# A denser order of the side work in a two-lane schedule, and a gate multiplied in another order

## The chip, the cores and the metric

One core of a Trainium2 chip runs the whole program in one launch. The metric is the device time of that launch in microseconds (us). TensorE multiplies, VectorE and ScalarE do the elementwise work, GpSimd a little of it, and SyncE issues the loads of the weights.

## The reference

Four layers over one sequence of 256 tokens with 2048 features, all in float32. The change touches the last of them (called layer 3 here), which reads, cut to its core:

```python
def odd_layer(x, norm_g, w_in, ...):
    proj = rmsnorm(x, norm_g) @ w_in
    xc, zc, qd, kd, vd, zd, a_pre, b_pre = split_cols(proj, OD_SIZES)
    xconv = causal_dwconv(xc.astype(f32), conv_c_w.astype(f32)) + conv_c_b.astype(f32)
    yc = rg_lru(xconv, gate_w, gate_b, lam) * jax.nn.silu(zc.astype(f32))
    qkv = jax.nn.silu(causal_dwconv(jnp.concatenate([qd, kd, vd], axis=-1).astype(f32), conv_d_w.astype(f32)))
...
    q = l2norm(q.reshape(b, s, H_D, HD_D))
    k = l2norm(k.reshape(b, s, H_D, HD_D))
...
    od = gated_delta_chunkwise(q, k, v, beta, g)
    yd = rmsnorm(od, onorm_g).reshape(b, s, W_D) * jax.nn.silu(zd.astype(f32))
    y = jnp.concatenate([yc, yd], axis=-1).astype(x.dtype)
    return y @ w_out

def rg_lru(xconv, gate_w, gate_b, lam):
...
    log_a = -C_RG * r * jax.nn.softplus(-lam.astype(jnp.float32))
    a = jnp.exp(log_a)
    inp = jnp.sqrt(-jnp.expm1(2.0 * log_a)) * (i * xconv)
...
    _, hs = lax.associative_scan(combine, (a, inp), axis=1)
```

The convolutions have four taps. `gated_delta_chunkwise` needs the inverse of a lower triangular matrix; the kernel gets it in blocks of 128 by six levels of doubling. silu(z) is computed as z/2 * (1 + tanh(z/2)). The result of the layer is added to x.

## The kernel before, in words

**The projections.** Every large product is done in three passes to hold float32 accuracy: the weights are split by ScalarE into a high part (a cast, line 1099) and by VectorE into a low part (a subtraction, line 1659, which waits for the cast), and TensorE multiplies high by high, high by low and low by high (lines 557 to 559). One weight tile of 128x1024 is a *half*; TensorE does 12 matmuls of 512 columns per half, in four triples. In layer 3 there are twelve projections of 32 triples each (384 triples), then the last product.

**The side work.** All else of layer 3 is written as generators, one per engine, that yield between their steps. TensorE's loop calls `next(side)` after each triple; ScalarE's and VectorE's loops call it four times per half too. The calls are numbered, here called places; a step named for place p is issued by every engine at place p of its own instruction order. There is no other order than this written one: an engine that has to wait at a step waits with all that it has behind it, the casts and subtractions for the projections included. Those are issued three halves ahead of their use (`AHEAD = 3`), at every fourth place.

**The lanes.** `lanes` (line 99) starts the generators: three lists of (place, generator), and an entry starts when its place is reached and the entry before it in its list has ended. The first list holds the gates' vectors, lru(0), lru(2), delta(0), delta(2); the second lru(1), lru(3), delta(1), delta(3); the third the four parts of the gate, gated(0) to gated(3), which only VectorE runs. Each list has its own buffers (`Lane`) and two PSUM banks. Within a generator, `to(step)` yields until that step. `wide_steps(lane)` stretches the steps of an lru by 4/3 in the first lane and by 6/3 in the second, rounded down; an lru has 32 steps. A delta has 115.

**An lru's steps** (its line on each engine): transposes at 0 (TensorE); copy at 1, first tap at 3 (ScalarE, 1491 and 1496); three tap pairs at 4, 6 and 8 (VectorE, 2124); the gate product "g" at 11 (TensorE, 953); two Tanh pairs at 12, two Exp pairs "A" at 15, Tanh "th" at 18, Sqrt at 23 (ScalarE, 1505, 1517, 1517, 1521; Tanh and Exp share a function table, Sqrt has another); products at 15 and 20, product and two scans at 25 (VectorE, 2141, 2146, 2150, 2154); transposes "st" at 28 (TensorE, 959); a copy to y at 30.

**A delta's steps:** transposes of q, k, v at 0 and 4 (597), copies and first taps on ScalarE from 0 to 7 (1537, 1546), nine tap pairs on VectorE from 4 to 22, the three Tanh at 10, 16 and 24 (1562); squares at 23 and their sums "ss" by one-column matmuls at 27 (987); a decay product at 30 (993), the decay block on VectorE at 32 (2193 to 2196), its exponentials at 34 (1568), u at 36 (2210); k times k at 42 (1002), "ad" at 43 and 45 (six of line 2220), q times k at 48 (1008), "tq" at 49 (2225, 2226), the transposes at 53 (1015) and 56, six levels of two steps each three places apart (972 on TensorE, 2233 on VectorE, 1580 and 1583 on ScalarE); u0, a10, u1 and o from 96 to 105 (1038 to 1055), and the normalized result to y by 114 (2261).

**Arrivals.** At the end of each projection ScalarE copies the result out of PSUM (line 1205, or 1639 for the gate's Tanh), between the side steps of two halves: x at places 32 and 64, q and k at 96, 160, 192 and 256, v at 128 and 224, z at 288, 320, 352 and 384. The projections alternate between two pairs of PSUM banks; `free` says what TensorE waits for before it overwrites a pair.

Of the kernel before, what the change touches and what calls it, by code (L numbers as in the profile page):

```python
# [10 lines left out]
ALU = mybir.AluOpType  # L11
# [72 lines left out]
def wide_steps(lane):  # L84

    to = steps()
    return lambda step: to(step * (4, 6)[lane] // 3)
# [71 lines left out]
def build_program(nc, a, out, layers=(0, 1, 2, 3)):  # L159
    assert tuple(layers) == (0, 1, 2, 3)  # L160
    ctx = ExitStack()
    with ctx:
# [107 lines left out]
        z3_a, z3_d = marks("z3_a", "tanh"), marks("z3_d", "z mul")  # L270
# [274 lines left out]
        def tensor(pe):  # L545
# [418 lines left out]
            def delta(pair):  # L964
# [34 lines left out]
                yield from to(42)  # L999
# [5 lines left out]
                yield from to(48)  # L1005
# [5 lines left out]
                yield from to(53)  # L1011
# [5 lines left out]
                yield from to(56)  # L1017
# [6 lines left out]
                for l in range(1, 7):  # L1024
                    yield from to(53 + 6 * l)
                    pe.wait_ge(*da.at(r, f"mt{l - 1}"))
                    four_by_four(b, v.AD, v.Mt).then_inc(*dp.up(f"z{l}"))
                    yield from to(56 + 6 * l)
# [11 lines left out]
                yield from to(99)  # L1040
# [4 lines left out]
                yield from to(102)  # L1045
# [4 lines left out]
                yield from to(105)  # L1050
# [8 lines left out]
                yield from to(115)  # L1059

            def delta_gates():
# [18 lines left out]
                    qk3_a.at(2, "qk"), v3_a.at(1, "v"), qk3_a.at(3, "qk"), z3_d.at(0, "z"), z3_d.at(1, "z")]  # L1080
# [5 lines left out]
            last_product(3, side, [yt_d.at(29, "lo"), z3_d.at(3, "z")], [], [z3_d.at(3, "mul")], fine=True)  # L1086


        def scalar(act):
# [438 lines left out]
            def delta(pair):  # L1528
# [41 lines left out]
                yield from to(53)  # L1570
# [3 lines left out]
                yield from to(56)  # L1574
                act.wait_ge(*dp.at(r, "mt"))
                act.copy(flat(v.Mt), ps[:, b, :]).then_inc(*da.up("mt0"))
                for l in range(1, 7):
                    yield from to(56 + 6 * l)
# [5 lines left out]
                yield from to(107)  # L1584
                act.wait_ge(*dd.at(r, "od"))
                act.activation(v.B, v.Z, ACT.Square).then_inc(*da.up("osq"))
                yield from to(115)
# [63 lines left out]
        def vector(dve):  # L1651
# [506 lines left out]
            def delta(pair):  # L2158
# [53 lines left out]
                for hh, bank in ((0, b + 1), (1, b)):  # L2212
                    yield from to(43 + 2 * hh)
# [9 lines left out]
                yield from to(49)  # L2223
# [3 lines left out]
                yield from to(50)  # L2227
                dve.wait_ge(*dg.at(r, "diag"))
                dve.tensor_tensor(v.M, v.AD, bc(L3.lev[:, 0], 1, 4), ALU.mult).then_inc(*dd.up("m"))
                for l in range(1, 7):  # L2230
                    yield from to(53 + 6 * l)
# [4 lines left out]
                yield from to(96)  # L2236
                dve.wait_ge(*dp.at(r, "u0"))
                dve.tensor_copy(v.u[:, :, 0], two(b)).then_inc(*dd.up("u0"))
                yield from to(99)
                dve.wait_ge(*dp.at(r, "a10"))  # L2240
                dve.tensor_tensor(v.u[:, :, 1], v.u[:, :, 1], two(b + 1), ALU.subtract).then_inc(*dd.up("a10"))
                yield from to(102)
                dve.wait_ge(*dp.at(r, "u1"))
                dve.tensor_copy(v.u[:, :, 1], two(b)).then_inc(*dd.up("u1"))
                yield from to(105)
# [3 lines left out]
                yield from to(109)  # L2249
# [4 lines left out]
                yield from to(112)  # L2254
                dve.wait_ge(*dg.at(r, "opow"))
                dve.tensor_tensor(v.Z, v.Z, bc(sc[:, 28:32], 2, P), ALU.mult).then_inc(*dd.up("on"))
                yield from to(114)
# [6 lines left out]
                yield from to(115)  # L2264
# [64 lines left out]
            def gated(n):  # L2329
# [15 lines left out]
                m.then_inc(*z3_d.up("mul"))  # L2345

# [6 lines left out]
        def gpsimd(pool):  # L2353
# [109 lines left out]
            def delta(pair):  # L2463
# [9 lines left out]
                yield from to(46)  # L2473
# [3 lines left out]
                yield from to(110)  # L2477
                pool.wait_ge(*dd.at(r, "omean"))
                pool.tensor_tensor(sc[:, 28:32], sc[:, 28:32], nhalf[:, 0:4], ALU.pow).then_inc(*dg.up("opow"))
                yield from to(115)  # L2480
# [52 lines left out]
```

## Time and profile before

| | |
|---|---|
| median of 3 runs | 2524.33 us (2523.95 to 2525.02) |
| profiled execution | 2524.33 us, its span 2522.6 us |
| mean granted TensorE clock | 0.991 |
| TensorE busy | 2470.3 us |
| VectorE, ScalarE, GpSimd busy | 1382.7, 1233.0, 125.0 us |
| layer 3's projections | from 2031.66 us on |

Times are from the span's start. "Busy" for TensorE counts pipelined matmuls, whose ends are modelled; a matmul of 512 columns is listed with 0.39 us though the next starts 0.23 us after it. What an engine waited for is inferred from semaphores.

### The profile page before, as it was taken

What the parts mean: (1) busy time and instruction counts of PE and PEld (TensorE: products, weight loads), DVE (VectorE), ACT (ScalarE), POOL (GpSimd) and SP (SyncE); (2) the same over time, 40 slices, a digit from 0 to 9 for tenths busy, and PEclk for the clock granted to TensorE, in tenths of its full rate; (3) what the DMA queues carried; (4) which work ended last, traced back from release to release, by engine and by line L of the source; (5) the groups of instructions that cost most, each with busy time, mean ns of one, the idle gap of its engine ahead of it and who ended that gap; (6) DMA issues with size and microseconds to landing.
All of it is one profiled execution on the core that took longest, in us unless ns stands there. A gap on an engine that the chain in (4) does not pass through costs nothing.

```text
span 2522.6 us, 30023 instructions
## 1 busy us (share of the span) xinstructions
PE 2470.3 (98%) x12030; PEld 2060.6 (82%) x12030; DVE 1382.7 (55%) x1848; ACT 1233.0 (49%) x1661; POOL 125.0 (5%) x125
## 2 busy tenths in 40 slices
PE   8999999999999999989999989999999999999999
PEld 6888888888888888868888868888888887888887
DVE  5645454645464646554545565555445466746554
ACT  4454444444454445344555345555444368645443
POOL 1101010101010101000000000000000000000000
PEclk9999999999999999989999989999999999999999
DMA  7545555555555554635533545555555555433344
GB/s 239 188 159 185 166 184 167 181 164 173 171 172 175 183 167 151 217 125 187 180 117 116 186 143 177 174 184 173 182 173 164 179 184 161 137 103 117 101 134 134
DMA packets 342048, 414.49 MB, mean 164 GB/s; under 512 B 19019, under 2 KB 269093, under 8 KB 341397
## 3 DMA queue, kind: packets, MB, share of 16 engines
q1 hardware_dynamic: 340500, 405.63, 50.3%
q0 software_dynamic: 1408, 6.94, 0.7%
q8 instruction: 95, 1.56, 0.3%
q14 instruction: 45, 0.36, 0.0%
HBM read 410.42 MB, written 2.10 MB: 164 GB/s over the span
## 4 chain that ended last, share of the span: by engine, by line
PE 92%; DVE 3%; ACT 3%; issue 1%; SPq 0%; DMA 0%; POOL 0%; DVEq 0%; ACTq 0%
PE ps L557 26%; PE ps L559 26%; PE ps L558 26%; PE ps L972 2%; PE ps L597 2%; PE ps L712 1%; DVE wlo L1659 1%; ACT whi L1099 1%; PE ps L699 1%; PE ps L773 1%; PE ps L704 1%; PE ps L772 1%; PE ps L785 0%; PE ps L696 0%; DVE x L1758 0%
## 5 line engine op out<-in xcount | busy, mean ns | idle before, releaser
L1659 DVE TENSOR_TENSOR wlo<-raw,whi 128x1024 fp32r<-128x1024 f32 (+1 forms) x774 | 950.3, 1233 | 858.0 <-ACT whi L1099 854.8
L557 PE MATMUL ps<-whi,xh 128*128 128x512 f32 (+1 forms) x3072 | 1227.4, 400 | 6.7 <-DVE wlo L1659 6.7
L559 PE MATMUL ps<-whi,xl 128*128 128x512 f32 (+1 forms) x3072 | 1198.0, 390 | 0.0
L558 PE MATMUL ps<-wlo,xh 128*128 128x512 f32 (+1 forms) x3072 | 1195.8, 389 | 0.0
L1099 ACT CAST whi<-raw 128x1024 fp32r<-128x1024 f32 (+1 forms) x774 | 801.6, 1041 | 771.3 <-PE ps L559 766.7
L557 PEld LDWEIGHTS ps<-whi,xh 128*128 128x128 f32 x3072 | 578.6, 188 | 123.0 <-issue 12.2
L559 PEld LDWEIGHTS ps<-whi,xl 128*128 128x128 f32 x3072 | 577.6, 188 | 120.4
L558 PEld LDWEIGHTS ps<-wlo,xh 128*128 128x128 f32 x3072 | 578.9, 188 | 109.7
L1177 ACT ACTIVATE work<-work,small 128x128 f32<-128x128 f32 (+1 forms) x80 | 46.1, 577 | 155.7 <-DVE small L1769 155.7
L2387 POOL TENSOR_TENSOR work<-work 128x512 f32<-128x512 f32 x48 | 77.0, 1605 | 872.4 <-DVE work L1844 488.6
L972 PEld LDWEIGHTS ps<-work 128*128 128x128 f32 x544 | 67.7, 191 | 6.1 <-DVE work L2233 2.6
L972 PE MATMUL ps<-work 128*128 128x128 f32 x544 | 68.7, 275 | 1.3 <-DVE work L2233 1.2
L1240 ACT COPY work<-ps 128x512 f32<-128x512 f32 x48 | 28.2, 587 | 65.0 <-PE ps L597 65.0
L597 PE MATMUL ps<-ident,x 128*128 128x128 f32 x128 | 25.7, 377 | 31.0 <-DVE x L1758 17.7
L1766 DVE CUSTOM_DVE_ANT_0 work<-ps,work 128x128 f32<-128x128 f32 (+1 forms) x80 | 38.2, 514 | 31.3 <-PE ps L699 17.5
L597 PEld LDWEIGHTS ps<-ident,work 128*128 128x128 f32 x352 | 42.8, 140 | 9.6
L597 PE MATMUL ps<-ident,work 128*128 128x128 f32 x352 | 50.4, 272 | 0.0
L597 PEld LDWEIGHTS ps<-ident,x 128*128 128x128 f32 x128 | 22.0, 198 | 34.7 <-DVE x L1758 27.3
L1279 ACT COPY work<-ps 128x1024 f32<-128x1024 f32 x32 | 32.4, 1012 | 27.4 <-PE ps L559 27.4
L1205 ACT ACTIVATE work<-ps,rstd 128x512 f32<-128x512 f32 (+3 forms) x56 | 28.3, 561 | 29.2 <-PE ps L559 28.6
L1183 ACT COPY work<-ps 128x384 f32<-128x384 f32 (+1 forms) x40 | 29.5, 736 | 26.3 <-PE ps L704 17.4
L2124 DVE SCALAR_TENSOR_TENSOR work<-work,vec 128x256 f32<-128x256 f32 x96 | 41.9, 480 | 0.3
(366 smaller groups left out, 1319.9 us busy)
## 6 DMA issues: line engine op xcount, KB each, us to landing
raw<-in_dsa_w_in SPq DMA_DIRECT2D x320, 512.0 KB, 4.5
raw<-in_ev_w_in SPq DMA_DIRECT2D x144, 512.0 KB, 4.6
raw<-in_od_w_in SPq DMA_DIRECT2D x96, 512.0 KB, 4.5
raw<-in_mla_w_in SPq DMA_DIRECT2D x48, 512.0 KB, 4.3
raw<-in_dsa_w_out SPq DMA_DIRECT2D x32, 512.0 KB, 4.6
raw<-in_mla_w_out SPq DMA_DIRECT2D x32, 512.0 KB, 4.7
raw<-in_ev_w_out SPq DMA_DIRECT2D x32, 512.0 KB, 4.6
raw<-in_od_w_out SPq DMA_DIRECT2D x32, 512.0 KB, 4.9
```

Source lines behind the costliest of these rows:

```text
L557: pe.matmul(o, xh[:, k, tokens[tb]], hi, start=start and s + l == 0, stop=False)
L558: pe.matmul(o, xh[:, k, tokens[tb]], lo, start=False, stop=False)
L559: m = pe.matmul(o, xl[:, k, tokens[tb]], hi, start=False, stop=stop and s + l == 2)
L597: m = pe.transpose(ps[:, bank, i * P:(i + 1) * P], src(i // 2, i % 2), ident[:, :])
L972: m = pe.matmul(ps[:, bank, n * P:(n + 1) * P], left[:, n, :], right[:, n, :], start=True, stop=True)
L1099: act.copy(whole_half(whi[:, h % 4], widths[u]), whole_half(raw[:, u % 4, 2 * (h % 2):2 * (h % 2) + 2], widths[u])).then_inc(hi_done, 1)
L1177: m = act.activation(w, w, ACT.Exp, bias=nb[:, tb:tb + 1], scale=scale, accum_out=den[:, tb:tb + 1])
L1279: act.copy(L0.h[:, 2 * s:2 * s + 2].rearrange("p b t c -> p t b c"), ps[:, b:b + 2, :].rearrange("p t (b c) -> p t b c", b=2)).then_inc(*e ...
L1659: dve.tensor_tensor(whole_half(wlo[:, h % 4], n), whole_half(raw[:, h // 2 % 4, 2 * (h % 2):2 * (h % 2) + 2], n), whole_half(whi[:, h % 4] ...
L1766: m = dve.tensor_tensor_reduce(w_, s_, m_, 1.0, LOWEST, ALU.add, ALU.max, mx[:, tb:tb + 1])
L2124: return dve.scalar_tensor_tensor(out=out_, in0=src[:, L3.PAD - 3 + j:L3.PAD - 3 + j + S], scalar=w, in1=out_, op0=ALU.mult, op1=ALU.add)
L2387: pool.tensor_tensor(L0.t1, L0.h[:, blk].rearrange("p t (h d) -> p (t h) d", h=2), L0.cosa, ALU.mult).then_inc(*p0_g.up(f"cos{n}"))
```

## The change

Four edits, all in layer 3, none of which changes what is computed:
- the second lane's lru is stretched by 5/3 instead of 6/3 (53 places instead of 64), and its two start at 44 and 101 instead of 48 and 114;
- in every delta, the steps after 36 are moved forward: by 2 from the product of k and k on, by 3 from the q and k transposes through the levels, by 4 from u0 on, so that it has 111 places;
- delta(1), delta(2) and delta(3) start at 164, 244 and 276 instead of 180, 250 and 298;
- the gate: before, (tanh + 1) * z goes to a scratch tile and is then multiplied by hrstd and y, one token block at a time. After, (tanh + 1) * y is written to y, and then z out of PSUM is multiplied by hrstd and y. PSUM is so released by the last operation instead of the first, and the Tanh's scratch tile by the first instead of the last. The extra delay of 25 places ahead of gated(3)'s last operations goes.

```diff
-    return lambda step: to(step * (4, 6)[lane] // 3)
+    return lambda step: to(step * (4, 5)[lane] // 3)
...
-    lane = [[(0, gates()), (40, lru(0)), (86, lru(2)), (132, delta(0)), (250, delta(2))],
-            [(48, lru(1)), (114, lru(3)), (180, delta(1)), (298, delta(3))],
+    lane = [[(0, gates()), (40, lru(0)), (86, lru(2)), (132, delta(0)), (244, delta(2))],
+            [(44, lru(1)), (101, lru(3)), (164, delta(1)), (276, delta(3))],
...
-                yield from to(42)
+                yield from to(40)
                 pe.wait_ge(*dd.at(r, "u"))
...
-                yield from to(48)
+                yield from to(46)
                 pe.wait_ge(*dd.at(r, "ad1"))
...
-                yield from to(53)
+                yield from to(50)
                 pe.wait_ge(*dd.at(r, "tq"))
...
-                    yield from to(53 + 6 * l)
+                    yield from to(50 + 6 * l)
...
-                yield from to(96)
+                yield from to(92)
...
-                yield from to(115)
+                yield from to(111)
...
-                    qk3_a.at(2, "qk"), v3_a.at(1, "v"), qk3_a.at(3, "qk"), z3_d.at(0, "z"), z3_d.at(1, "z")]
+                    qk3_a.at(2, "qk"), v3_a.at(1, "v"), qk3_a.at(3, "qk"), z3_d.at(0, "mul"), z3_d.at(1, "mul")]
...
-                    act.wait_ge(*z3_d.at(turn - 1, "mul"))
+                    act.wait_ge(*z3_d.at(turn - 1, "add"))
...
-                dve.wait_ge(*z3_a.at(n, "tanh"))
-                dve.scalar_tensor_tensor(out=L3.scratch, in0=L3.scratch, scalar=1.0, in1=ps[:, b:b + 2, :],
-                                         op0=ALU.add, op1=ALU.mult).then_inc(*z3_d.up("z"))
-                yield from turns(25 if n == 3 else 1)
                 for i in range(2):
                     dve.wait_ge(*(rg_a[i].at(n, "end") if n < 2 else dl_d[i].at(n - 2, "fin")))
-                dve.wait_ge(*z3_d.at(n, "z"))
+                dve.wait_ge(*z3_a.at(n, "tanh"))
+                dve.scalar_tensor_tensor(out=y[:, :, c], in0=L3.scratch, scalar=1.0, in1=y[:, :, c],
+                                         op0=ALU.add, op1=ALU.mult).then_inc(*z3_d.up("add"))
                 for tb in range(TB):
                     yield
-                    m = dve.scalar_tensor_tensor(out=y[:, tb, c], in0=L3.scratch[:, tb], scalar=hrstd[:, tb:tb + 1],
+                    yield
+                    dve.wait_ge(*z3_d.at(n, "add"))
+                    m = dve.scalar_tensor_tensor(out=y[:, tb, c], in0=ps[:, b + tb, :], scalar=hrstd[:, tb:tb + 1],
                                                  in1=y[:, tb, c], op0=ALU.mult, op1=ALU.mult)
-                    yield
                 m.then_inc(*z3_d.up("mul"))
+                yield
```

The steps of ScalarE, VectorE and GpSimd in a delta are moved by the same numbers as TensorE's.

## Rows read from the trace of the kernel before

**Rows 1.** the page: span, and busy time of each engine with its share
```profile
span 2522.6 us, 30023 instructions
...
PE 2470.3 (98%) x12030; PEld 2060.6 (82%) x12030; DVE 1382.7 (55%) x1848; ACT 1233.0 (49%) x1661; POOL 125.0 (5%) x125
```

**Rows 2.** TensorE waits of layer 3: line waited for, total us, times, longest
```profile
PE ps L953 <- DVE work L2124: 2.4, 2, 1.2
PE ps L1008 <- DVE work L2220: 2.1, 1, 2.1
PE ps L987 <- ACT work L1559: 1.4, 1, 1.4
PE ps L1055 <- DVE work L2244: 1.2, 1, 1.2
PE ps L972 <- DVE work L2233: 1.2, 2, 0.6
```

**Rows 3.** timeline of TensorE: start us, us, instruction, idle before in brackets
```profile
2079.01 0.39 PE L557 MATMUL ps<-whi,xh 128*128 128x512 f32 x1
...
2085.13 1.99 PE L953 MATMUL ps<-work 128*128 128x256 f32 x8 [1.20 <-DVE work L2124]
...
2091.09 0.39 PE L557 MATMUL ps<-whi,xh 128*128 128x512 f32 x1
...
2092.18 0.66 PE L959 MATMUL ps<-ident,work 128*128 128x128 f32 x4 [0.25 <-DVE work L2154]
...
2192.29 0.48 PE L557 MATMUL ps<-whi,xh 128*128 128x512 f32 x1
```

**Rows 4.** timeline of ScalarE between places 56 and 72
```profile
2075.18 1.28 ACT L1505 ACT_TABLE_LOAD   x1
2076.47 0.47 ACT L1505 ACTIVATE work<-ps,work 128x256 f32<-128x256 f32 x1
...
2078.85 2.09 ACT L1517 ACTIVATE work<-work 128x256 f32<-128x256 f32 x4
2080.83 1.26 ACT L1205 ACTIVATE work<-ps,rstd 128x512 f32<-128x512 f32 x2
...
2082.91 1.11 ACT L1517 ACTIVATE work<-work 128x256 f32<-128x256 f32 x2
...
2084.97 1.28 ACT L1521 ACT_TABLE_LOAD   x1
```

**Rows 5.** timeline of VectorE, same stretch
```profile
2088.99 1.23 DVE L1659 TENSOR_TENSOR wlo<-raw,whi 128x1024 fp32r<-128x1024 f32 x1 [2.18 <-ACT whi L1099]
...
2090.86 1.27 DVE L2154 TENSOR_TENSOR_SCAN work<-work 128x256 f32<-128x256 f32 x2
```

**Rows 6.** busy time by stretch; the column after POOL is the granted clock
```profile
2160.30:2163.70 3.40, 3.40 (x10) 2.20 (x8) 1.93 (x4) 3.30 (x4) 0.60 (x1) 0.54 0.22 84
```

**Rows 7.** VectorE groups by form from 2028 to 2470 us
```profile
L1659 DVE TENSOR_TENSOR wlo<-raw,whi 128x1024 fp32r<-128x1024 f32 x112 | 137.3, 1226 | 121.3 <-ACT whi L1099 120.3 <-DVE work L2334 0.4
L2124 DVE SCALAR_TENSOR_TENSOR work<-work,vec 128x256 f32<-128x256 f32 x96 | 41.9, 480 | 0.3
...
L2220 DVE SCALAR_TENSOR_TENSOR work<-ps,small,work 128x128 f32<-128x128 f32 x24 | 6.8, 343 | 2.4 <-PE ps L1003 2.4
L2342 DVE SCALAR_TENSOR_TENSOR y<-work,hrstd,y 128x512 f32<-128x512 f32 x8 | 6.0, 746 | 0.1
...
L2154 DVE TENSOR_TENSOR_SCAN work<-work 128x256 f32<-128x256 f32 x8 | 5.1, 679 | 0.1
L2334 DVE SCALAR_TENSOR_TENSOR work<-work,ps 128x1024 f32<-128x1024 f32 x4 | 4.8, 1212 | 0.0
```

**Rows 8.** ScalarE groups by form from 2028 to 2470 us
```profile
L1099 ACT CAST whi<-raw 128x1024 fp32r<-128x1024 f32 x113 | 118.7, 1050 | 99.5 <-PE ps L559 99.0
...
L1546 ACT ACTIVATE work<-work,vec 128x256 f32<-128x256 f32 x24 | 10.5, 506 | 0.0
...
L1568 ACT ACTIVATE work<-work 128x128 f32<-128x128 f32 x16 | 5.9, 391 | 1.4 <-DVE work L2196 1.4
```

More of the change, by code:

```diff
@@ L269, in build_program @@
         x3_a, qk3_a, v3_a = marks("x3_a", "x"), marks("qk3_a", "qk"), marks("v3_a", "v")
-        z3_a, z3_d = marks("z3_a", "tanh"), marks("z3_d", "z mul")
+        z3_a, z3_d = marks("z3_a", "tanh"), marks("z3_d", "add mul")
         rg_a = [marks(f"rg_a{i}", "cp c0 gate A asq th sqrt end") for i in range(2)]
@@ L1016, in delta @@
                 m.then_inc(*dp.up("tr"))
-                yield from to(56)
+                yield from to(53)
                 pe.wait_ge(*da.at(r, "st"))
@@ L1024, in delta @@
                 for l in range(1, 7):
-                    yield from to(53 + 6 * l)
+                    yield from to(50 + 6 * l)
                     pe.wait_ge(*da.at(r, f"mt{l - 1}"))
                     four_by_four(b, v.AD, v.Mt).then_inc(*dp.up(f"z{l}"))
-                    yield from to(56 + 6 * l)
+                    yield from to(53 + 6 * l)
                     pe.wait_ge(*dd.at(r, f"z{l}"))
@@ L1039, in delta @@
                 m.then_inc(*dp.up("u0"))
-                yield from to(99)
+                yield from to(95)
                 pe.wait_ge(*dd.at(r, "u0"))
@@ L1044, in delta @@
                 m.then_inc(*dp.up("a10"))
-                yield from to(102)
+                yield from to(98)
                 pe.wait_ge(*dd.at(r, "a10"))
@@ L1049, in delta @@
                 m.then_inc(*dp.up("u1"))
-                yield from to(105)
+                yield from to(101)
                 pe.wait_ge(*dd.at(r, "u1"))
@@ L1085, in tensor @@
                         then=turning_y(3, [[z3_d.at(2, "mul")], [], [], [], [], []]) if n == 11 else None)
-            last_product(3, side, [yt_d.at(29, "lo"), z3_d.at(3, "z")], [], [z3_d.at(3, "mul")], fine=True)
+            last_product(3, side, [yt_d.at(29, "lo"), z3_d.at(3, "mul")], [], [z3_d.at(3, "mul")], fine=True)
         def scalar(act):
@@ L1569, in delta @@
                 m.then_inc(*da.up("ex"))
-                yield from to(53)
+                yield from to(50)
                 act.wait_ge(*dp.at(r, "tr"))
@@ L1573, in delta @@
                 act.copy(v.TRN[:, 1], ps[:, b, :]).then_inc(*da.up("st"))
-                yield from to(56)
+                yield from to(53)
                 act.wait_ge(*dp.at(r, "mt"))
@@ L1577, in delta @@
                 for l in range(1, 7):
-                    yield from to(56 + 6 * l)
+                    yield from to(53 + 6 * l)
                     act.wait_ge(*dp.at(r, f"t{l}"))
@@ L1583, in delta @@
                         act.copy(flat(v.M), ps[:, b + 1, :]).then_inc(*da.up(f"m{l}"))
-                yield from to(107)
+                yield from to(103)
                 act.wait_ge(*dd.at(r, "od"))
                 act.activation(v.B, v.Z, ACT.Square).then_inc(*da.up("osq"))
-                yield from to(115)
+                yield from to(111)
             def delta_gates():
@@ L2212, in delta @@
                 for hh, bank in ((0, b + 1), (1, b)):
-                    yield from to(43 + 2 * hh)
+                    yield from to(41 + 2 * hh)
                     if hh == 0:
@@ L2222, in delta @@
                     m.then_inc(*dd.up(f"ad{hh}"))
-                yield from to(49)
+                yield from to(47)
                 dve.wait_ge(*dp.at(r, "qk"))
@@ L2226, in delta @@
                 dve.tensor_tensor(v.TRN[:, 1, P:], ps[:, b, 0:3 * P], v.E[:, 1], ALU.mult).then_inc(*dd.up("tq"))
-                yield from to(50)
+                yield from to(48)
                 dve.wait_ge(*dg.at(r, "diag"))
@@ L2230, in delta @@
                 for l in range(1, 7):
-                    yield from to(53 + 6 * l)
+                    yield from to(50 + 6 * l)
                     dve.wait_ge(*dp.at(r, f"z{l}"))
@@ L2248, in delta @@
                                   ALU.mult).then_inc(*dd.up("od"))
-                yield from to(109)
+                yield from to(105)
                 dve.wait_ge(*da.at(r, "osq"))
@@ L2253, in delta @@
                 dve.tensor_scalar(sc[:, 28:32], sc[:, 24:28], 1.0 / P, EPS, ALU.mult, ALU.add).then_inc(*dd.up("omean"))
-                yield from to(112)
+                yield from to(108)
                 dve.wait_ge(*dg.at(r, "opow"))
                 dve.tensor_tensor(v.Z, v.Z, bc(sc[:, 28:32], 2, P), ALU.mult).then_inc(*dd.up("on"))
-                yield from to(114)
+                yield from to(110)
                 dve.wait_ge(*dd.at(r, "on"))
@@ L2263, in delta @@
                                   ALU.mult).then_inc(*dd.up("fin"))
-                yield from to(115)
+                yield from to(111)
             def delta_gates():
@@ L2472, in delta @@
                 pool.tensor_tensor(sc[:, 0:8], sc[:, 0:8], nhalf[:, 0:8], ALU.pow).then_inc(*dg.up("pow"))
-                yield from to(46)
+                yield from to(44)
                 pool.wait_ge(*dd.at(r, "ad1"))
@@ L2476, in delta @@
                                    pattern=[[0, 4], [-1, P]], channel_multiplier=1).then_inc(*dg.up("diag"))
-                yield from to(110)
+                yield from to(106)
                 pool.wait_ge(*dd.at(r, "omean"))
                 pool.tensor_tensor(sc[:, 28:32], sc[:, 28:32], nhalf[:, 0:4], ALU.pow).then_inc(*dg.up("opow"))
-                yield from to(115)
+                yield from to(111)
             run(lanes(lambda: nothing, delta, lru, lambda n: nothing))
```

8 lines of the change are left out of this document (4 added, 4 removed).

## The prediction

> **What bounds the kernel now.** I read the page first: TensorE is busy for 2470.3 of 2522.6 us [rows 1]. The change adds and removes no TensorE instruction, so it can move the time only through TensorE's waits and its clock. The profiled execution took 2524.33 us, its span and 1.73 us around it; that is also the median of the three runs, so no correction is needed.
>
> Next come TensorE's waits in layer 3, the only layer that is touched. They add up to 8.3 us in five lines of the view [rows 2]; shorter ones, the 0.25 of L959 in [rows 3] among them, bring them to 8.9 us. The reader is to see that each is a wait for a small VectorE or ScalarE result that a side chain delivers late. The third thing is the clock. Behind the 1.4 us wait for the squares (L987), TensorE shows a granted clock of 0.54 for 3.4 us [rows 6]: it ran at 1.2 GHz where it otherwise runs at 2.4, which costs about half of 3.4, or 1.6 us. So at most 8.9 + 1.6 = 10.5 us can be won, and what can be lost has no such bound.
>
> How the side chains are paced: a *place* is what lies between two triples of projection matmuls. A triple takes 0.68 us (2091.09 begins triple 77; L959 follows it after one triple and a wait of 0.25) [rows 3], so four places, one half, take 2.72 us plus side matmuls. I write T(n) for the start of triple n; T(64) is 2079.01 [rows 3]. In each half ScalarE owes a cast of 1.05 us [rows 8] and VectorE a subtraction of 1.23 us that waits for that cast [rows 7]. Everything else is in the engines' program order around these, so a ScalarE backlog reaches every later VectorE operation through the subtraction: its 112 instances waited 120 us for the cast [rows 7].
>
> **The change part by part.** The four edits are: the lru lanes 1 take 53 instead of 64 places and start at 44 and 101 (were 48 and 114); each delta takes 111 places (was 115); the second delta of a pair starts 32 places behind the first (was 48); and the gate is multiplied in another order.
>
> *Gate.* It stays one 128x1024 operation of 1.21 us and two of 128x512 of 0.75 us [rows 7]. TensorE's wait for bank release moves from the first to the last of them, four places later. At place 294 that is 26 places ahead of its use at 320. Cost zero; if that cover were gone it would be at most 0.75 + 0.75 us. The 25-place delay of the fourth gate goes, but TensorE shows no wait at its late transposes (place 424) before, so nothing is won there. The order of the Tanh and the last multiplication also shows no wait now. Zero.
>
> *Place 77, lru(0) with lru(1).* Before, ScalarE does at places 56 to 70: table load and gates of lru(0) (ends 2078.0), cast, A of lru(0), arrival of x, cast, th, cast, then table load and sqrt, which ends at about 2086.9 [rows 4]. Now lru(1) has its gate product at place 62, its gates at 64 and its A at 69, in front of that sqrt. T(64) becomes 2079.01 + 1.9 (the eight gate matmuls, L953 [rows 3]) = 2080.9. ScalarE, full throughout: th(0) ends 2084.1, gates(1) +1.5 = 2085.6, cast 2086.6, A(1) +2.0 = 2088.6 (four L1517 [rows 4]), sqrt(0) +1.9 = 2090.5, cast of place 72: 2091.5. Before, the chain from the start of VectorE's subtraction (2088.99) to TensorE's release (2092.18) took 3.2 us: subtraction, product, two scans [rows 3, 5]. So it is released at 2094.7. It gets there at 2080.9 + 14 x 0.68 = 2090.4. Wait: 4.3 us, where 1.2 + 0.25 stood.
>
> *Place 100, lru(2).* Arrival of qk, cast, subtraction, taps are unchanged; only lru(1)'s sqrt no longer sits in front (it held the arrival for 0.45 us). 1.17 becomes 0.75.
>
> *Place 147, lru(3) with delta(0).* Count from T(120) = 0, when lru(3)'s gate product is done. ScalarE: gates 2.4, cast 3.8 (not before T(124) = 2.7), end(2) 4.4, A(3) 6.4, arrival of v 7.9, cast 8.9, th(3) 9.9, cast 10.9, two copies 11.9, four first taps at 0.4 apiece 13.5 [rows 8], cast 14.5, copy and taps of v 15.9, table load and sqrt 17.8, cast 18.9. VectorE: subtraction 20.05, two tap pairs of 0.8 (two L2124 overlap) 21.65, product and scans 1.9 [rows 7] = 23.5. TensorE: 28 places x 0.68 = 19.0, plus st(2), eight and four transposes (0.55 + 0.95 + 0.5) = 21.05. Wait: 2.4 us. What is behind the waiting instruction on TensorE is its whole projection.
>
> *Places 159 to 178.* Following the same queues, delta(0)'s squares come 0.4 us late (1.4 before), its decay product waits 1.3 us for VectorE's subtraction behind the arrival of qk. Then delta(1), now starting at 164, brings its taps into delta(0)'s middle. In program order ScalarE has from T(164): cast 1.05, two copies 2.2; the exponentials cannot start before VectorE's decay block (3.3) and take 1.9 (six L1568 [rows 8]) = 5.25; four taps 6.9; cast 8.0. VectorE: subtraction 9.2, u 9.8. TensorE asks for u at place 40 of the delta (was 42), at 8.1 to 8.4: wait 1.4 to 1.7, I take 1.4. Two taps pairs, subtraction, taps and six L2220 later, ad1 ends 0.8 us behind the request. Sum 0.4 + 1.3 + 1.4 + 0.8 = 3.9; the 0.16 for lru(3) at place 171 goes.
>
> *Places 276 to 304.* The second pair meets the same, and gated(0) at 290 falls between delta(2)'s ad1 and its tq. From place 276 to 300 VectorE owes: 6 subtractions at 1.15 = 6.9; delta(3)'s nine tap pairs 7.2 and two products 1.2; delta(2)'s decay block, scalings and u 2.1, six ad 1.7, tq and m 1.5; the gate 2.5: 23.1 us. TensorE needs 24 x 0.68 = 16.3 and about 5 of side matmuls, 21.3. Placed in order, the waits are 1.4 (u), 0.9 (ad1), 1.4 (tq, behind the 1.2 us gate) and 1.1 (the first level). Sum 4.8, where 2.1 stood (L1008) [rows 2].
>
> *The rest.* The 1.2 for u1 behind the subtraction (L1055) and the two of 0.6 for the levels (L972) have equivalents after, but one of the 0.6 is already counted in the 1.1 above: 2.4 before, 1.8 after.
>
> Sum of waits after: 4.3 + 0.75 + 2.4 + 3.9 + 4.8 + 1.8 = 17.95; before 8.9: +9.05. Clock: the dip of 1.6 us at 2160 stood behind a wait and sixteen one-column matmuls; with a wait of 0.4 there I let it go: -1.6. A 4.3 us wait at place 77 may draw one of its own (the 2.1 us wait drew none), unknown from the rows: 0 to 1.6, I take 0. Total +7.45 us: **2531.8**. Bounds: with every overlap of queues a little kinder (each new wait down by two thirds) it is about +1; with two dips of 1.6 +10.7.
>
> One rule speaks for a higher price. In the rows a switch of ScalarE's functions costs 1.28 us and the activation starts 0.01 us behind the load (2075.18 + 1.28 to 2076.47) [rows 4]. The Trainium skill ("ScalarE: Activation LUTs", What ACT_TABLE_LOAD costs) says that each switch has a drain besides and comes to about 2.66 us. By that, the two switches ahead of place 77 and the two ahead of 147 would each add up to 1.4 us and the forecast would be some 5 us more, as an estimate; the trace contradicts it, so it is not in the sum.
>
> **The rivals.**
> *A. The backlogs are absorbed (no change).* The side work has slack: before, VectorE idled 121 us in front of its subtractions [rows 7]. If my queues are each 1.5 to 2 us too pessimistic, seven waits shrink to about the old 9 us and the time is 2522 to 2527. Against it: ScalarE's 56 to 72 is an ordered queue with no idle between 2075 and 2087 [rows 4], and 3.5 us are inserted in it.
> *B. Faster.* The collisions of before go: lru(3)'s tail no longer lies on delta(0) at 160 to 171 (1.4 + 0.2 + the 1.6 of clock), the gate no longer on delta(1)'s end at 290 to 299 (2.1), u1 (1.2). With new waits under 1.5 us in all: 2524.3 - 6.5 + 1.3 = about 2519. It decides if the new overlaps at 69 and 284 fit; my tables say they don't.
> *C. The clock falls.* Waits of 4.3 and 2.4 us in succession draw two or more dips of 1.6 us, and they are not hidden: 2535 and above.
>
> **How the numbers follow.** A measurement of this kernel tells about 0.2% (5 us) from no change. Forecast (2528 to 2535): 0.56. A: 0.27. B: 0.11. C: 0.06. The range that leaves out no more than 2 in 10 takes in A and most of the forecast: 2522 to 2536; the forecast's own is 2528 to 2535. The forecast of 7.5 us lies 2.5 above the bound, so a little of it counts as the same: slower 0.59, same 0.30, faster 0.11.
>
> **What would show it.** In the profile after: a wait of 3.5 to 5 us of L959 for L2154 near 2090; one of 1.5 to 3.5 us of L959 near 2150; waits of L1002 for L2210 and of L1008 for L2220 in both pairs, L1015 for L2226 near 2310; no 1.2 GHz stretch near 2160; no wait on y or z. It is wrong if the sum of TensorE's waits in layer 3 is below 12 us, above all if ScalarE runs sqrt(0) before 2089.

## The result and the profile after

The changed kernel takes 2545.61 us (median of 4, 2540.57 to 2546.34) against 2524.59 us: ratio 1.0078, 95% interval 1.0066 to 1.009. (The ratios in this document come with the runs. They are not the quotient of the two medians, which is 1.0083 here; the two differ by up to 0.0008.) It is slower by 21 us, where 2531.8 us (range 2522 to 2536) had been forecast. The profiled execution has a span of 2544.0 us.

The page of the changed kernel, the lines that answer to [rows 1]:

```profile
span 2544.0 us, 30020 instructions
...
PE 2480.8 (98%) x12030; PEld 2067.7 (81%) x12030; DVE 1382.0 (54%) x1848; ACT 1232.2 (48%) x1661; POOL 123.7 (5%) x125
```

The same 12030 matmuls, but TensorE's busy time grew by 10.5 us. Waiting cannot do that; slower matmuls can. Its waits in layer 3, the view of [rows 2] (waiting line, releaser, us in total, times, longest):

```profile
PE ps L959 <- DVE work L2154: 6.6, 2, 4.2
PE ps L972 <- DVE work L2233: 3.5, 2, 2.3
PE ps L1002 <- DVE work L2210: 3.1, 2, 1.9
PE ps L1043 <- DVE work L2238: 2.1, 2, 1.5
PE ps L1015 <- DVE work L2226: 1.2, 1, 1.2
PE ps L953 <- DVE work L2124: 0.9, 1, 0.9
PE ps L597 <- DVE y L2342: 0.9, 1, 0.9
...
PE ps L987 <- ACT work L1559: 0.3, 1, 0.3
PE ps L1008 <- DVE work L2220: 0.3, 1, 0.3
```

These are 18.9 us against 8.9 before: +10.0. The clock is the other half. Busy time by stretch of the changed kernel, for the four stretches of layer 3 in which the column after POOL, the granted clock, stands at half:

```profile
2093.40:2100.30 6.90, 4.74 (x13) 3.89 (x14) 3.90 (x6) 3.23 (x6) 0.00 (x0) 0.51 0.48 152
2168.50:2175.30 6.80, 6.80 (x17) 4.32 (x16) 1.90 (x3) 1.61 (x2) 2.08 (x2) 0.50 0.50 157
2322.10:2325.50 3.40, 3.40 (x11) 2.75 (x10) 3.40 (x8) 0.57 (x1) 0.00 (x0) 0.51 0.82 292
2346.00:2356.20 10.20, 10.20 (x42) 9.33 (x40) 2.00 (x3) 2.12 (x3) 2.03 (x1) 0.50 0.32 103
```

TensorE is busy for 4.74 + 6.80 + 3.40 + 10.20 = 25.1 us of them at 1.2 instead of 2.4 GHz, which costs half of it, 12.6 us. Before there was one such stretch of 3.4 us [rows 6], worth 1.7. So +10.9 us, and with the waits +20.9; the spans differ by 21.4, of which 0.95 stood before layer 3 began.

The place of the largest wait, read as in [rows 3 to 5]: TensorE, ScalarE and VectorE of the changed kernel (start, us, instruction, idle before it).

```profile
2081.71 0.39 PE L557 MATMUL ps<-whi,xh 128*128 128x512 f32 x1
...
2095.56 1.11 PE L959 MATMUL ps<-ident,work 128*128 128x128 f32 x4 [4.17 <-DVE work L2154]
...
2096.90 0.63 PE L558 MATMUL ps<-wlo,xh 128*128 128x512 f32 x1
```

```profile
2084.01 1.09 ACT L1517 ACTIVATE work<-work 128x256 f32<-128x256 f32 x2
2085.00 0.47 ACT L1505 ACTIVATE work<-ps,work 128x256 f32<-128x256 f32 x1
...
2087.36 2.10 ACT L1517 ACTIVATE work<-work 128x256 f32<-128x256 f32 x4
2089.48 1.28 ACT L1521 ACT_TABLE_LOAD   x1
2090.77 0.63 ACT L1521 ACTIVATE work<-work 128x512 f32<-128x512 f32 x1
```

```profile
2092.37 1.22 DVE L1659 TENSOR_TENSOR wlo<-raw,whi 128x1024 fp32r<-128x1024 f32 x1 [3.01 <-ACT whi L1099]
...
2094.23 1.27 DVE L2154 TENSOR_TENSOR_SCAN work<-work 128x256 f32<-128x256 f32 x2
```

Up to here the whole program lies 0.95 us later than before; all of that stood already at layer 3's first triple (2032.61 instead of 2031.66), so it is not the work of the moved steps. ScalarE does th(0), at once the gates of lru(1), the cast, and four exponentials, and only then loads the table for sqrt(0), at 2089.48 where before it did so at 2084.97 [rows 4]. VectorE's subtraction of place 72 starts at 2092.37, the scans follow, and TensorE is released at 2095.56 after 4.17 us; the forecast was 4.3. The clock fell at 2093.4, about 2 us into the wait. The matmul at 2096.90 shows what comes with it: 0.63 us instead of 0.39. The wait of 2.38 us at place 147 drew no such stretch.

The stretch at 2168.5 has no such wait near it. TensorE's timeline there:

```profile
2165.58 1.95 PE L987 MATMUL ps<-ones,work 128*128 128x1 f32 x16 [0.34 <-ACT work L1559]
2167.39 0.48 PE L557 MATMUL ps<-whi,xh 128*128 128x512 f32 x1
...
2169.12 0.63 PE L557 MATMUL ps<-whi,xh 128*128 128x512 f32 x1
...
2170.53 2.07 PE L993 MATMUL ps<-work,ident 8*128 8x256 f32 x4
```

It waited only 0.34 us, then did sixteen matmuls of one column, and about a microsecond later the clock was at half. That asks whether waits or small matmuls lower the clock.

### The profile page after: what moved, and what is told of

Read it like the earlier page. It is cut to its first block, busy times and chain, and to the rows that moved or that the text cites. A ratio compares the mean times of both kernels' runs of the same rounds, so it can differ in the third digit from the quotient of the medians.

```text
span 2544.0 us, 30020 instructions
## 1 busy us (share of the span) xinstructions
PE 2480.8 (98%) x12030; PEld 2067.7 (81%) x12030; DVE 1382.0 (54%) x1848; ACT 1232.2 (48%) x1661; POOL 123.7 (5%) x125
## 4 chain that ended last, share of the span: by engine, by line
PE 90%; DVE 4%; ACT 3%; issue 1%; DMA 0%; SPq 0%; POOL 0%; ACTq 0%; DVEq 0%
PE ps L557 26%; PE ps L559 26%; PE ps L558 26%; PE ps L972 2%; PE ps L597 2%; DVE wlo L1659 1%; PE ps L712 1%; ACT whi L1099 1%; PE ps L699 1%; PE ps L773 1%; PE ps L704 1%; DVE work L2124 1%; PE ps L772 1%; PE ps L785 0%; PE ps L696 0%
## 5 line engine op out<-in xcount | busy, mean ns | idle before, releaser
L972 PEld LDWEIGHTS ps<-work 128*128 128x128 f32 x544 | 69.1, 195 | 8.3 <-DVE work L2233 4.7
L972 PE MATMUL ps<-work 128*128 128x128 f32 x544 | 70.2, 279 | 3.5 <-DVE work L2233 3.5
L597 PE MATMUL ps<-ident,x 128*128 128x128 f32 x128 | 25.1, 367 | 31.5 <-DVE x L1758 17.7
L597 PEld LDWEIGHTS ps<-ident,x 128*128 128x128 f32 x128 | 21.1, 192 | 35.3 <-DVE x L1758 27.3
```

The lines of the kernel that those rows point to most:

```text
L597: m = pe.transpose(ps[:, bank, i * P:(i + 1) * P], src(i // 2, i % 2), ident[:, :])
L972: m = pe.matmul(ps[:, bank, n * P:(n + 1) * P], left[:, n, :], right[:, n, :], start=True, stop=True)
```

## The experiments

Theory W: the loss is 10 us of waits, made by what ScalarE's and VectorE's written order puts in front of the releasing operation (Q), and 11 us of clock that these waits draw. Rival D: crowded small matmuls lower the clock, whether or not TensorE waits. Each kernel is compared with the kernel before on the same chip; its median there was 2524.8 to 2526.1 us, so times of two experiments can differ by 1.3 us from the chip alone.

**1. The gate alone.** The new order of multiplications in parts 0 to 2 of the kernel before, part 3 as before.

```diff
-                dve.scalar_tensor_tensor(out=L3.scratch, in0=L3.scratch, scalar=1.0, in1=ps[:, b:b + 2, :],
-                                         op0=ALU.add, op1=ALU.mult).then_inc(*z3_d.up("z"))
...
+                dve.scalar_tensor_tensor(out=y[:, :, c], in0=L3.scratch, scalar=1.0, in1=y[:, :, c],
+                                         op0=ALU.add, op1=ALU.mult).then_inc(*z3_d.up("add"))
```

> The kernel before with the new order of the gate's multiplications in parts 0 to 2 (part 3 as before, since its first operation would otherwise wait for results that come later in VectorE's own order). Theory W (the 21 us are 10 us of new TensorE waits and 12 us of half clock drawn by them): the gate has no share, 2524.6 +/- 1 us, the waits of layer 3 near 8.9 us and one short stretch at 1.2 GHz. Rival G (PSUM released four places later holds a projection up): a wait on y of 1 us or more at places 320 or 352 and a time over 2526.

Measured: 2525.76 us, ratio 0.9998 (0.9989 to 1.0008); waits 8.7 us, no wait on y at 320 or 352. G falls. The profile has a second 3.4 us stretch at half clock near place 299, behind a wait (L1008, 1.9 us; 2.1 before) that drew none in the profile before, so such stretches differ between executions.

**2. The lru's lane alone.**

```diff
-    return lambda step: to(step * (4, 6)[lane] // 3)
+    return lambda step: to(step * (4, 5)[lane] // 3)
-            [(48, lru(1)), (114, lru(3)), (180, delta(1)), (298, delta(3))],
+            [(44, lru(1)), (101, lru(3)), (180, delta(1)), (298, delta(3))],
```

> The kernel before with the second lane's lru alone changed (5/3, starts 44 and 101). Theory W: waits of 4.2 us at place 77 and 2.4 at place 147 appear, 1.4 at 160 shrinks, and the clock falls to 1.2 GHz behind them for two stretches of 3 to 7 us: 2524.6 + 7.5 to 10, about 2531 to 2534. Rival D (the clock falls only where both lanes' small matmuls lie close together, mostly after place 160): the same waits but at most one short stretch, about 2528.

Measured: 2532.75 us, ratio 1.002 (1.001 to 1.003). Its waits on TensorE:

```profile
PE ps L959 <- DVE work L2154: 6.5, 2, 4.2
...
PE ps L987 <- ACT work L1559: 0.4, 1, 0.4
```

They are 4.16 us at place 77, 2.32 at 147 and 0.36 at 159. There are two stretches of 6.8 us at half clock, at the first and behind the third; the 2.32 us wait drew none. A third of the loss is here.

**3. Offset 48 between the deltas of a pair**, with the new lru and the new steps, and the old gate (the gate's lines are undone too).

```diff
-            [(44, lru(1)), (101, lru(3)), (164, delta(1)), (276, delta(3))],
+            [(44, lru(1)), (101, lru(3)), (180, delta(1)), (292, delta(3))],
```

> The changed kernel with the second delta of each pair 48 places behind the first instead of 32 (starts 180 and 292), and the old gate, which that needs. Theory W: the waits at 173, 192, 285, 295 and 304 (about 8 us) go or shrink to 3, and with them the two stretches at 1.2 GHz from 2320 on; the lru's share stays: 2532 to 2535. Rival S (the delta's own shorter steps make the waits, whatever the offset): waits of 5 us or more after place 160 remain, time over 2538.

Measured: 2533.88 us, ratio 1.0026 (1.0016 to 1.0037). After place 160 there are nine short waits, 0.4 to 0.9 us each, 5.0 us in all, and no half clock behind them. That sum is the sign that rival S named, but the kernel before has 4.9 us there too, against 11.0 in the changed kernel, and the time is under S's 2538: S falls. Over experiment 2 the shorter steps cost about 1 us, which is within the noise; the offset of 32 costs the rest: 2545.6 - 2533.9 = 11.7 us (the gate's order, which differs too, has no share, see 11).

**4. The changed kernel with its waits filled** by matmuls whose results nobody reads.

```diff
+            def fill(bank, n):
+                for _ in range(n):
+                    pe.matmul(ps[:, bank, :], xh[:, 0, 0:P], flat(xh[:, 0:2, :]), start=True, stop=True)
...
                 yield from to(28)
+                if pair in (0, 3):
+                    pe.wait_ge(*rg_a[i].at(r, "gate"))
+                    fill(b + 1, 18 if pair == 0 else 10)
                 pe.wait_ge(*rg_d[i].at(r, "scan"))
```

> The changed kernel with useless 512-column matmuls put where TensorE waits: 18 at place 77, 10 at 147, 5 and 8 ahead of the product of k and k in delta(0) and delta(2), 5 and 10 ahead of their first level. They fill about as long as the waits last. Theory W: the clock stays at 2.4 GHz at most of these places, time at 1.2 GHz in layer 3 falls from 27 us to 10 or less, the time to 2533 to 2539. Rival D (crowded small matmuls, not waits, lower the clock): the stretches at 1.2 GHz stay, 2545 or more.

The other fills stand ahead of L1002 and of the first level. Measured: 2537.21 us, ratio 1.0041 (1.0026 to 1.0056), 8.4 us less than the changed kernel with 56 more matmuls. Granted clock by stretch in this kernel, the place of the old 4.2 us wait and the one behind place 160:

```profile
2093.40:2100.30 6.90, 6.81 (x32) 5.38 (x31) 5.28 (x7) 4.86 (x7) 0.10 (x1) 1.00 0.46 152
2165.50:2168.90 3.40, 3.40 (x10) 2.65 (x9) 2.01 (x4) 1.55 (x3) 0.44 (x1) 0.52 0.27 105
```

The first is back at 2.4 GHz, and so are the two of the second pair; only 3.4 us behind the one-column matmuls are left. So in the three other places it took an idle TensorE to draw the half clock; the fourth fits rival D.

**5. The stretch of 5/3 with the old starts** (48 and 114).

```diff
-    return lambda step: to(step * (4, 6)[lane] // 3)
+    return lambda step: to(step * (4, 5)[lane] // 3)
```

> The kernel before with the stretch of 5/3 alone, the lru starts left at 48 and 114. Then only lru(1)'s gates (1.5 us), not its A (2.0 us), come in front of sqrt(0) in ScalarE's order. Theory Q (each wait is what ScalarE's and VectorE's written order puts in front of the releasing operation): the wait at place 77 is 4.2 - 2.0 = 2.2 us, the one at 147 moves to 160 with 1.5 to 3 us; time 2 to 5 us over before. Rival P (the shorter stretch itself leaves an lru too few places for its chain): the wait stands at lru(1)'s own steps, places 90 or later.

Measured: 2528.98 us, ratio 1.0007 (0.9998 to 1.0016). Waits:

```profile
PE ps L987 <- ACT work L1559: 3.5, 1, 3.5
...
PE ps L959 <- DVE work L2154: 1.9, 1, 1.9
```

The wait at 77 is 1.91 us, where taking the 2.0 us of exponentials out of ScalarE's way had forecast 2.2; the other moved to place 159 and is 3.5, above the 1.5 to 3 expected. Q holds, P falls.

**6. gated(0) at 304 in the changed kernel.**

```diff
-            [(290, gated(0)), (322, gated(1)), (354, gated(2)), (388, gated(3))]]
+            [(304, gated(0)), (322, gated(1)), (354, gated(2)), (388, gated(3))]]
```

> The changed kernel with gated(0) started at place 304 instead of 290. Theory Q: VectorE's 2.5 us of gate leave the rush of delta(2) and delta(3); the waits at 295 (1.2) and 304 (2.3) become those of the first pair, where no gate lies (0 and 1.15), so 2 to 3 us less of waits, and with the second pair's waits like the first's the clock falls for one stretch less; 2538 to 2543. Rival: the rush is set by ScalarE (exponentials and taps) and nothing changes, 2545.

Measured: 2537.27 us, ratio 1.0042 (1.0029 to 1.0054). The level waits (L972) come to 2.3 us, 1.15 in either pair, and L1015 waits no more: 2.4 us less, as Q said. In all the waits are 3.8 us less; the rest is the first pair's 1.25 us at L1002, which has nothing to do with the gate: it seems hidden because the half clock behind place 160 lasts 10.2 us in this profile, not 6.8, and makes TensorE late. The second pair's 10.2 us at half clock are gone, the 3.4 us ahead of them stay. The time lies just under the 2538 to 2543 expected: the collision of the gate with the pair is worth 8 us of the medians, more than its waits.

**7. A delay alone.** Six useless products before lru(0)'s scan, in the kernel before.

```diff
+                if pair == 0:
+                    for n in range(6):
+                        dve.tensor_tensor(flat(v.gt), flat(v.A2), flat(v.A2), ALU.mult).then_inc(dly, 1)
+                        dve.wait_ge(dly, n + 1)
                 dve.wait_ge(*ra.at(r, "sqrt"))
```

> The kernel before with six useless 128x512 VectorE products (0.7 us each, 4.1 in all, into a tile that is free) in front of lru(0)'s scan, and the order otherwise as before. It makes the wait at place 77 near 4 us without any crowding of small matmuls. Theory W: the clock falls to 1.2 GHz behind it, for one stretch of 3 to 7 us, costing 1.7 to 2.4 us beyond the wait; time +4 to +6.5 over before. Rival D: no stretch behind place 77, time +4 or less.

Measured: 2531.71 us, ratio 1.0019 (1.001 to 1.0028). The wait (L960 in this kernel's lines), and the stretch that TensorE resumes in:

```profile
PE ps L960 <- DVE work L2159: 4.6, 1, 4.6
```

```profile
2097.60:2101.00 3.40, 2.97 (x9) 2.56 (x10) 2.09 (x3) 0.00 (x0) 0.00 (x0) 0.52 0.00 0
```

TensorE stood still from 2093.42 to 2098.03 with only 512-column matmuls in the 4 us before, and the clock fell at about 2097.7. So a wait suffices, without small matmuls crowded about it. It fell about 4 us into this wait, and about 2 us into the one of 4.17 us in the changed kernel. The decay product waits too now, for 0.8 us. This profile has a third stretch of 3.4 us, at the 2.1 us wait of L1008, as in experiment 1. The ratio is small beside 6.5 us of medians; the executions of the kernel before themselves spread from 2523.6 to 2530.5 us there, with mean clocks from 0.992 to 0.989.

**8. The gaps of the layer normalizations filled** in the kernel before (36 and 14 matmuls in each).

```diff
             def turn_x(layer):
                 for g in range(8):
+                    if layer in (1, 2) and g == 0:
+                        pe.wait_ge(*add_d.at(layer - 1, "add2"))
+                        fill(0, 36)
+                    if layer in (1, 2) and g == 4:
+                        pe.wait_ge(*xt_a.at(8 * layer, "hi"))
+                        fill(0, 14)
```

> The kernel before with useless 512-column matmuls in TensorE's two long gaps at the layer normalizations: 36 (8.2 us) in each gap of 8.4 us and 14 in each of 3.6 us. Theory W: the two stretches of 17.1 us at 1.2 GHz (at 1087 and 1476) disappear or fall below 7 us; since most of what runs in them is transposes that wait for ScalarE and VectorE anyway, the time falls by 2 to 5 us. Rival: the clock falls whatever fills the gap, time within 1 us of before.

Measured: 2525.85 us, ratio 0.9998 (0.9989 to 1.0007), mean clock 0.995 to 0.998. TensorE in the first gap, and below it the same transposes in the kernel before:

```profile
1085.80 8.32 PE L597 MATMUL ps<-xh 128*128 128x512 f32 x36
1094.40 1.10 PE L601 MATMUL ps<-ident,x 128*128 128x128 f32 x8 [0.28 <-DVE x L1768]
1096.79 1.09 PE L601 MATMUL ps<-ident,x 128*128 128x128 f32 x8 [1.30 <-DVE x L1768]
```

```profile
1093.80 1.97 PE L597 MATMUL ps<-ident,x 128*128 128x128 f32 x8 [8.43 <-DVE x L1758]
1096.19 1.97 PE L597 MATMUL ps<-ident,x 128*128 128x128 f32 x8 [0.43 <-DVE x L1758]
```

Both stretches of 17 us at half clock are gone and the eight transposes take 1.1 instead of 1.97 us, but the next group starts 2.39 us after the first in both kernels, when VectorE's quarter of x is there: what the matmuls gained, the wait took (1.30 instead of 0.43 us). The clock was low where it did not matter: the mechanism as said, the gain forecast not.

**9. gated(0) at 304 in the kernel before.** The edit is that of 6.

> The kernel before with gated(0) moved from place 290 to 304. Theory Q (what stands ahead in VectorE's written order makes the wait): the 2.1 us wait at place 299 falls below 1 us and nothing else moves; 1 to 1.5 us under before, more where it also spares a stretch at 1.2 GHz. Rival: the wait is set by delta(1)'s end and stays, no difference.

Measured: 2528.57 us, ratio 1.0004 (0.9995 to 1.0013). Waits:

```profile
PE ps L972 <- DVE work L2233: 3.9, 3, 2.7
...
PE ps L1008 <- DVE work L2220: 0.4, 1, 0.4
```

L1008 fell from 2.1 to 0.4 us, and a wait of 2.71 us appeared at place 313, where delta(3)'s taps now meet the gate. Between 2324.7 us and the operation it waits for (2335.3), VectorE's timeline holds four pairs of delta(3)'s taps, two subtractions and the gate's three operations. This wait has 3.4 us at half clock with it. The wait had moved, not gone; "nothing else moves" was wrong.

**10. The kernel before with gated(0) at 304, the filled gaps, and 5, 5 and 6 matmuls at places 71, 101 and 160.** The edits of 8 and 9, and:

```diff
                 yield from to(11)
+                if pair in (1, 2):
+                    fill(b + 1, 5)
                 pe.wait_ge(*rg_d[i].at(r, "conv"))
...
                 yield from to(27)
+                if pair == 0:
+                    pe.wait_ge(*da.at(r, "cp1"))
+                    fill(b + 1, 6)
                 pe.wait_ge(*da.at(r, "sq"))
```

> The kernel before with gated(0) at 304, useless matmuls in the two gaps of the layer normalizations, and 5, 5 and 6 of them at the waits of places 71, 101 and 160. Theory W: mean clock 0.998, no stretch at 1.2 GHz in layer 3 in most executions, so 2519 to 2523, and less spread between executions. Rival: the filled places cost as much as they give, 2524 to 2527.

Measured: 2523.34 us, ratio 0.9992 (0.9983 to 1.0). Within what can be told from no change, and above the 2519 to 2523 expected; the 2.7 us wait of 9 is here too, with 3.4 us at half clock.

**11. The changed kernel with the old gate.** Starts and steps stay as changed, the gate's lines in the diff ahead of the prediction are undone.

> The changed kernel with the old order of the gate, starts and steps as changed. It takes the new gate apart from the offset of 32. Theory Q: the waits are the changed kernel's within 1 us and so is the time, 2543 to 2547, since the gate's operations take the same VectorE time at nearly the same places. Rival G: the new gate has a large share of the 11.7 us that lie between the offsets 48 and 32, time under 2540.

Measured: 2545.71 us, ratio 1.0073 (1.0059 to 1.0088), waits 19.0 us, 27.3 us at half clock. The gate's new order has no share.

**12. The one-column matmuls twice**, in the kernel before.

```diff
-                for n, m_ in enumerate((v.M, v.Mt)):
+                for n, m_ in 2 * list(enumerate((v.M, v.Mt))):
```

> The kernel before with the sixteen one-column matmuls that sum the squares issued twice in every delta (places 159, 207, 277, 325). It adds four times 1.6 us of small matmuls without adding a wait. Theory W in its strict form (only idle TensorE lowers the clock): +6.4 us, no new stretch at 1.2 GHz at 207, 277 and 325; about 2531. Rival D (matmuls of one column do as little for the clock as none): a stretch of 3 to 7 us behind each, 2536 or more.

Measured: 2540.04 us, ratio 1.0053 (1.0037 to 1.0068). The profile is of the longest of four executions, 2545.5 us; the others took 2539.4 to 2540.4, so it shows more half clock than they had. The waits are 8.7 us, unchanged. The timeline of TensorE around place 207, where nothing waits, and the clock behind places 159, 207 and 277:

```profile
2218.57 4.83 PE L987 MATMUL ps<-ones,work 128*128 128x1 f32 x32
2223.26 0.77 PE L557 MATMUL ps<-whi,xh 128*128 128x512 f32 x1
```

```profile
2162.90:2176.60 13.70, 13.70 (x38) 10.31 (x38) 5.22 (x10) 5.83 (x9) 2.02 (x1) 0.51 0.26 77
2220.90:2227.70 6.80, 6.80 (x27) 6.22 (x28) 0.39 (x2) 0.00 (x0) 1.65 (x1) 0.51 0.48 154
2309.70:2316.50 6.80, 6.80 (x23) 5.47 (x24) 2.08 (x4) 1.04 (x1) 2.02 (x1) 0.51 0.00 0
```

The strict form of W falls: at 207 the clock fell some 2 us after the first of the 32 began, with no wait near. But not behind every group, as D had it. At place 325 the same 32 took 3.63 us and the clock stayed up, and so it did in the kernel before at the three groups of sixteen that had no wait right ahead of them (2211, 2294 and 2350 us; the first is shown):

```profile
2369.33 3.63 PE L987 MATMUL ps<-ones,work 128*128 128x1 f32 x32
```

```profile
2210.61 1.84 PE L987 MATMUL ps<-ones,work 128*128 128x1 f32 x16
```

At full clock the added sixteen cost 3.63 - 1.84 = 1.8 us, four times 7.2; the other half of the 14 us between the medians is clock.

**13. The one-column matmuls in two eights**, one triple apart, in the kernel before.

```diff
                 for n, m_ in enumerate((v.M, v.Mt)):
+                    if n:
+                        yield from to(28)
                     for k in range(4):
```

VectorE's operation that waits for them moves from step 28 to 29.

> The kernel before with the sixteen one-column matmuls of each delta issued as eight at place 27 and eight at place 28, with a triple of wide matmuls between. Theory D2 (the clock falls where TensorE has little to do for some microseconds, by waiting or by one-column matmuls): the stretch of 3.4 us near place 160 stays, since the 1.4 us wait is there too, but the executions with a mean clock of 0.989 become rarer, median 0.5 to 2 us under before. Strict theory W: no difference.

Measured: 2524.66 us, ratio 0.9999 (0.999 to 1.0009). No difference: the 3.4 us stretch stays, as expected, but the slower executions do not become measurably rarer, where theory D2, that a TensorE with little to do lowers the clock, had a median 0.5 to 2 us lower.

**14. The kernel before with the split, the filled gaps and the fills at 71, 101 and 160.** The edits of 8, 10 (without gated(0)) and 13 together.

> The kernel before with the split of e13, the filled gaps of e8 and the fills at places 71, 101 and 160. Theory D2: mean clock 0.998 or 0.999 in nearly every execution, no stretch at 1.2 GHz near place 160 or 208, 2519 to 2523. Strict theory W: like e10, 2523.3.

Measured: 2523.63 us, ratio 0.9989 (0.998 to 0.9998). The lowest ratio of all, by 0.1% under before and not measurably under 10; it misses the 2519 to 2523 of D2. Its profile has no half clock near 160 or 208, but still 3.4 us at the 2.1 us wait of L1008, which was not filled.

**15. The changed kernel, filled and split.** The edits of 4 and 13 together.

> The changed kernel with the fills of e4 and the split of e13. Theory D2: the last stretch at 1.2 GHz of layer 3, behind place 160, goes too: 2534 to 2536.5 where e4 had 2537.2. What then lies over before is the waits (or their filling) alone, about 10 us. Strict theory W: 2537 as e4.

Measured: 2535.74 us, ratio 1.004 (1.0027 to 1.0053). Layer 3 of this kernel and, below it, of the changed kernel (granted clock after POOL):

```profile
2028.00:2500.00 472.00, 463.98 (x2499) 391.81 (x2498) 280.22 (x437) 255.22 (x379) 16.98 (x21) 1.00 0.42 132
```

```profile
2028.00:2500.00 472.00, 453.06 (x2404) 382.61 (x2402) 275.96 (x436) 252.35 (x377) 17.51 (x24) 0.97 0.41 128
```

The column is rounded, so the places of the old stretches of this kernel are shown closer:

```profile
2162.00:2182.00 20.00, 18.14 (x96) 14.38 (x95) 10.40 (x20) 13.20 (x25) 2.08 (x2) 1.00 0.43 125
2318.00:2358.00 40.00, 38.32 (x217) 32.18 (x216) 27.24 (x51) 16.79 (x28) 2.66 (x2) 1.00 0.33 105
```

There is no half clock left in layer 3. That is what the split adds to 4; in time the two can't be told apart (ratios 1.0040 and 1.0041, on two chips). What remains over before is 10.9 us, near the 10.0 of new waits. It isn't an exact sum: before has 1.7 us of clock that this kernel hasn't, and the 7.7 us of waits left plus the 56 filling matmuls (an estimate at 0.23 us each: 12.7) are 1.5 us more than the 18.9 that they replace.

## Why the prediction was wrong, point by point

- *The waits* were right in mechanism and, with some luck, in sum: 18.9 us against 17.95 forecast. Place 77: 4.17 (4.3). Place 100: 0.94 (0.75). Place 147: 2.38 (2.4). Places 159 to 178: 0.34, 0, 1.25 and 0.28 (0.4, 1.3, 1.4, 0.8); the decay product did not wait, since half clock had made TensorE late; without half clock there, in 15, it waited 0.75. The second pair: 1.87, 0, 1.19 and 2.33 (1.4, 0.9, 1.4, 1.1). Not foreseen were 1.15 at the first pair's level and 0.57 and 1.51 at L1043, the latter where the end of delta(1) meets the taps of delta(2); "the rest" had 1.8 and was these and 0.9 on y, 4.1 in all. So 2.0 us too much at 159 to 178 and 2.9 too little in the second pair and the rest nearly cancelled.
- *The step that failed* is the clock: "A 4.3 us wait at place 77 may draw one of its own [...]: 0 to 1.6, I take 0" and, for the stretch at place 160, "with a wait of 0.4 there I let it go: -1.6". It measured 12.6 us in place of 0, a change of +10.9 instead of -1.6. Two things were wrong in it. I priced a stretch by the one row at hand (3.4 us, 1.6 us of cost), but they lasted up to 10.2 us. And I let the stretch at 160 go with its wait: it stood behind a wait *and* sixteen one-column matmuls, and with 0.34 us of wait left it came all the same, 6.8 us long. Experiment 12 shows that one-column matmuls can lower the clock by themselves when there are 32 of them. With the measured waits and clock in its sum the forecast would be 2524.3 + 10.0 + 10.9 = 2545.2, so no other term of size was missing.
- *Rival C* (2535 and above) had the right mechanism with a chance of 0.06 and a price of 1.6 us a stretch; it should have been in the range. Rivals A and B fell with the waits. (The 2.1 us wait at 299 that B puts down to delta(1)'s end belongs to delta(2), which started at 250 and does its product of q and k at step 48.)
- *The gate at no cost*: right (1 and 11). That it collides with the second pair was right as well, but with the clock the collision costs 8 us, not the 2.5 of its two waits (6).
- *The load of an activation table* costs 1.28 us in the changed kernel too (2089.48), with nothing behind it. The price of the Trainium skill ("ScalarE: Activation LUTs", What ACT_TABLE_LOAD costs) is again not what the trace shows.
- *The signs in the profile* came as listed, except the wait of L1008 for L2220 (0.28 us in one pair), the stretch at 1.2 GHz that was not to be there near 2160 (it came at 2168), a wait on y of 0.9 us, and L1015, which came at 2334 and not near 2310.

How far the slower shares of 2, 3 and 4 add up is open to about 2 us, as the stretches at half clock differ between executions: the changed kernel ran from 2538.6 to 2547.1 us over all its executions. What exactly decides whether such a stretch comes, where it begins and where it ends, the runs do not show.

## What to carry to other kernels

Where side work is issued at written places, a wait can be worked out from the queues within some tenths of a microsecond; do it for the engine that feeds the releaser (ScalarE's casts here), not only for the releaser. On a TensorE that is 98% busy, price new waits at one to two times their sum: 5.0 us of them cost 6.5 us in 7, 3.6 us cost 6.7 in 2 and 10.0 us cost 21 in the changed kernel. Look at runs of one-column matmuls beside a wait as if they were part of it. A wait that goes at one place may come back at the next, so add up the waits of the whole stretch.

## What the runs showed of the hardware that was not expected

- TensorE's clock fell to 1.2 GHz about 4 us into a wait of 4.6 us with no small matmuls near (7, for 3.4 us), and about 2 us into 32 one-column matmuls without any wait (12, place 207, for 6.8 us); the same 32 at place 325 left it at 2.4 GHz. 512-column matmuls in the waits kept it at 2.4 GHz (4, 15).
- The same wait does not always lower it. The one of L1008, 1.9 to 2.2 us, has 3.4 us at half clock with it in the profiles of 1, 7, 12 and 14, and none in those of before, 2, 5, 8 and 13. The one of 2.3 to 2.4 us at place 147 had none in the changed kernel, 2 and 6.
- The executions of the kernel before spread by 7 to 8 us (0.3%) on a chip, in step with a mean clock of 0.988 (2531.0 us) to 0.993 (2522.9 us).
- Keeping the clock up in the gaps of the layer normalizations (mean clock 0.995 to 0.998 instead of 0.989 to 0.992) was worth nothing that could be measured (8).
